# Cross attention with its scores two heads ahead of the transposes, and an output layer whose first block goes chunk by chunk

## The chip, the cores and the metric

One core of one Trainium2 chip runs the whole program in one launch. The metric is the device time of an execution in microseconds (us). The kernel before was timed three times; one more execution was recorded by the profiler.

## What is computed

The reference is a stack of two models over 512 tokens of width 1024. Each of the first model's two layers has a mixer, a cross attention over 256 memory rows, and a feed-forward part; the second model has two blocks of its own. The part that matters here is the cross attention, called once in each layer of the first model:

```python
def memory_cross_attention(h, mem_n, wq, wkv, wo):
    ...
    q = (h @ wq).reshape(B, S, XA_HEADS, XA_HEAD_DIM)
    k, v = jnp.split(mem_n @ wkv, 2, axis=-1)
    ...
    s = jnp.einsum('bshd,bmhd->bhsm', q, k).astype(jnp.float32) * (XA_HEAD_DIM ** -0.5)
    p = jax.nn.softmax(s, axis=-1).astype(v.dtype)
    return jnp.einsum('bhsm,bmhd->bshd', p, v).reshape(B, S, XA_WIDTH) @ wo

x = x + memory_cross_attention(rmsnorm(x, norm_xattn_g), mem_n, wq, wkv, wo)
```

## The kernel before

The program is a list of stages (`schedule`), and each engine runs its own function for each stage, in the order of the list. Engines meet only by semaphores. Around the change the list reads: the query layer (`xq`, two blocks), the attention (`xattn`, four heads), the output layer (`xo`, four blocks, which add to X), then the feed-forward part.

**Linear layers.** The activations lie with features on the partitions, in chunks of 128 features by 512 tokens. To keep float32 precision each operand is split into a hi and a lo part, and each product is three matmuls (`three`, L943 to L945): hi by hi, hi by lo, lo by hi. A block is 256 output features: two PSUM banks (m = 0, 1) of ACC, summed over the input chunks k. Blocks take turns on two pairs of banks, ACC[0:2] and ACC[2:4]. The weights arrive from memory in units of 1 MB over SP's queue (L841) into one of two RAW buffers; ACT makes the hi part (WH, L1620), VectorE (DVE) the lo part (WL, L2040). A unit of the output layer holds two of its blocks (`bpu` = 2), and its blocks are drained only when both are done (`unit_done`); DVE then adds them to X (L2119). The query layer's blocks are drained by DVE into XQ (L2097), 1024 values per partition at a time, which posts `block_done`.

A block normally runs over all k of bank 0 and then over all k of bank 1. The first block of a layer that opens behind a norm (`first_block`, L968 to L975) runs over k outside and the two banks inside, so that it can start on the first chunks. Either form waits for `h_ready` before it reads chunk k.

**Attention**, per head h, with the two buffers or bank pairs chosen by h % 2:

- scores (TensorE, L1075): four matmuls of 128x256 (the profile counts eight) into a pair of banks of ACC. For h = 0 it waits until both query blocks are drained; for h of 2 and 3 until the exponential has read the banks (`xs_exp`);
- maximum (DVE, L2291 and L2292), posts `xs_max`;
- exponential (ACT, L1738), four times 128x256 with a running sum, into XP, after the transposes of head h - 2 have read it (`xs_turned`);
- probabilities (DVE, L2297 and L2298): XP times the inverse of the sums, posts `xs_probs`;
- transposes (`turn`, TensorE, L1084): eight of 128x128 into the banks MIX[0:2], after the copy of head h - 1 has emptied them;
- copy (`copy_turned`, ACT, L1753) to XPT;
- output (TensorE, L1093): two matmuls (four in the profile) into MIX[2] or MIX[3];
- T (DVE, L2304), HH (`hi_chunks`, ACT, L1667) and HL (`lo`, DVE, L2308): the head's output as a chunk for the output layer, split in hi and lo; HL posts `h_ready`. T has two buffers, and the chunk after next waits until the lo part is made.

Each queue runs in the order written. Before, TensorE's is s0 s1 t0 s2 t1 o0 s3 t2 o1 t3 o2 o3 (s scores, t transposes, o output); ACT's is e0 e1 c0 e2 c1 hi0 e3 c2 hi1 c3 hi2 hi3 (e exponential, c copy); DVE's is m0 m1 p0 m2 p1 m3 p2 T0 lo0 p3 T1 lo1 T2 lo2 T3 lo3 (m maximum, p probabilities).

The MLA attention, elsewhere in the list, has eight heads in an order of the same kind: s0 s1 t0 s2 t1 o0 s3 t2 o1 and so on (L1492, L1506, L1515), with ten transposes a head.

Of the kernel before, what the change touches and what calls it, by code (L numbers as in the profile page):

```python
# [31 lines left out]
XH = 4  # L32
# [384 lines left out]
def build(nc, wall, xT, memT, params, consts, pos, poolw, params2, consts2, feats, decays, mats, filters, out):  # L417
# [7 lines left out]
    with ctx:  # L425
# [42 lines left out]
        T = place("T", [P, 2, S])  # L468
# [471 lines left out]
        def _(pe):  # L940
# [6 lines left out]
            def pe_linear(st):  # L947
# [4 lines left out]
                def period(i):  # L952
                    upp = 2 * st.upb
                    bpp = 2 * st.bpu
                    for j in in_period(st, i):
                        b = i * bpp + (st.b0 + j)
                        pair = (st.b0 + j) % 2
                        first_block = st.opens and isinstance(i, int) and i == j == 0
                        second_block = st.opens and isinstance(i, int) and i == 0 and j == 1
                        if not (isinstance(i, int) and b < 2):  # L960
                            pe.wait_ge(block_done, b - 1)
                        for q in range(st.upb):
                            ju = j * st.upb + q if st.bpu == 1 else j // st.bpu
                            n, add = unit_of(st, i, ju)
                            slot = n % 2
                            pe.wait_ge(w_lo, n + add + 1)
                            ks = range(8 * q, min(8 * q + 8, st.kc))
                            t0 = (j % st.bpu) * 2 * st.kc  # L968
                            if first_block and not tcs:
                                for k in ks:  # L970
                                    pe.wait_ge(h_ready, st.hin + k + 1)
                                    for m in range(2):
                                        c0 = (t0 + 2 * k + m) * P
                                        last = three(ACC[:, 2 * pair + m, :], WH[slot][:, c0:c0 + P], WL[slot][:, c0:c0 + P],
                                                     HH[:, k, :], HL[:, k, :], k == 0, k == st.kc - 1)  # L975
                            elif tcs:
                                for tc in range(tcs):
                                    if second_block and tc == 2:
                                        late_scale(st.norm)
                                    for k in ks:  # L980
                                        if tc == 0 and not st.whole:
                                            pe.wait_ge(h_ready, st.hin + k + 1)
                                        o = ACC[:, 2 * pair:2 * pair + 2, :].rearrange("p a (b n) -> p (a b) n", b=2)[:, tc]
                                        th, tl = HH[:, st.k0 + k, tc * P:tc * P + P], HL[:, st.k0 + k, tc * P:tc * P + P]
                                        c0 = (t0 + 2 * (k - 8 * q)) * P
                                        wh, wl = WH[slot][:, c0:c0 + 256], WL[slot][:, c0:c0 + 256]
                                        last = three(o, th, tl, wh, wl, k == 0, k == st.kc - 1)
                            else:
                                for m in range(1 if st.half and isinstance(i, int) and i * bpp + j == st.nb - 1 else 2):
                                    if second_block and m == 1:  # L990
                                        late_scale(st.norm)
                                    for k in ks:
                                        if m == 0 and src_h is HH and not st.whole:
                                            pe.wait_ge(h_ready, st.hin + k + 1)
                                        if m == 0 and src_h is HIDH:
                                            pe.wait_ge(hid_ready, st.hidin + k + 1)
                                        c0 = (t0 + 2 * (k - 8 * q) + m) * P
                                        last = three(ACC[:, 2 * pair + m, 0:width],
                                                     WH[slot][:, c0:c0 + P], WL[slot][:, c0:c0 + P],
                                                     src_h[:, st.k0 + k, 0:width], src_l[:, st.k0 + k, 0:width],  # L1000
                                                     k == 0, k == st.kc - 1)
                            if j % st.bpu == st.bpu - 1:
                                last.then_inc(unit_done, 1)
                        if first_block and st.norm.own == 2:
                            sum_paired(st.norm)
# [59 lines left out]
            def pe_xattn(st):  # L1065
                o = st.nth * XH

                def scores(h):
                    if h == 0:
                        pe.wait_ge(block_done, st.b0)  # L1070
                    if h >= 2:
                        pe.wait_ge(xs_exp, o + h - 1)
                    for tc in range(TC):
                        dst = ACC[:, 2 * (h % 2):2 * (h % 2) + 2, :].rearrange("p a (b n) -> p (a b) n", b=2)[:, tc]
                        mm = pe.matmul(dst, XQ[:, h, tc * P:tc * P + P], XK[:, h, :], start=True, stop=True)  # L1075
                    mm.then_inc(xs_scores, 1)

                def turn(h):
                    pe.wait_ge(xs_probs, o + h + 1)
                    if h >= 1:  # L1080
                        pe.wait_ge(xs_copied, o + h)
                    for mc in range(MC):
                        for tc in range(TC):
                            mm = pe.transpose(MIX[:, mc, tc * P:tc * P + P],  # L1084
                                              XP[:, h % 2, tc, mc * P:mc * P + P], ident)
                    mm.then_inc(xs_turned, 1)

                def output(h):
                    pe.wait_ge(xs_copied, o + h + 1)
                    if h >= 2:  # L1090
                        pe.wait_ge(t_ready, st.h0 + h - 1)
                    for mc in range(MC):
                        mm = pe.matmul(MIX[:, 2 + h % 2, :], XV[:, mc, h * P:h * P + P], XPT[:, h % 2, mc, :],  # L1093
                                       start=(mc == 0), stop=(mc == MC - 1))
                    mm.then_inc(xs_out, 1)

                scores(0)
                for h in range(XH):
                    if h + 1 < XH:
                        scores(h + 1)  # L1100
                    turn(h)
                    if h:
                        output(h - 1)
                output(XH - 1)

            def pe_prep(st):
                L = st.layer
# [502 lines left out]
        def _(act):  # L1610
# [118 lines left out]

            def act_xattn(st):  # L1730
                o = st.nth * XH
                for h in range(XH):
                    act.wait_ge(xs_max, o + h + 1)
                    if h >= 2:
                        act.wait_ge(xs_turned, o + h - 1)
# [2 lines left out]
                        a = act.activation(XP[:, h % 2, tc, :], src, ACT.Exp, bias=XS[:, h % 2, 0, tc:tc + 1],  # L1738
                                           scale=float(P) ** -0.5, accum_out=XS[:, h % 2, 1, tc:tc + 1])
                    a.then_inc(xs_exp, 1)  # L1740
                    if h:
                        copy_turned(st, h - 1)
                    if h >= 2:
                        hi_chunks(st.h0 + h - 2, [h - 2])
                copy_turned(st, XH - 1)
                hi_chunks(st.h0 + XH - 2, [XH - 2, XH - 1])

            def copy_turned(st, h):
                o = st.nth * XH
# [284 lines left out]
        def _(v):  # L2034
# [250 lines left out]
            def dve_xattn(st):  # L2285
                o = st.nth * XH

                def maximum(h):
                    v.wait_ge(xs_scores, o + h + 1)
                    src = ACC[:, 2 * (h % 2):2 * (h % 2) + 2, :].rearrange("p a (b n) -> p (a b) n", b=2)  # L2290
                    step(v.tensor_reduce(XS[:, h % 2, 2, :], src, AX.X, ALU.max))  # L2291
                    v.tensor_scalar(XS[:, h % 2, 0, :], XS[:, h % 2, 2, :], -float(P) ** -0.5, None, ALU.mult)\  # L2292
                        .then_inc(xs_max, 1)
# [12 lines left out]
                def lo(c):  # L2306
                    v.wait_ge(h_hi, st.h0 + c + 1)
                    v.tensor_tensor(HL[:, c, :], T[:, (st.h0 + c) % 2, :], HH[:, c, :], ALU.subtract).then_inc(h_ready, 1)  # L2308

                maximum(0)  # L2310
                for h in range(XH):
                    if h + 1 < XH:
                        maximum(h + 1)
                    probs(h)
                    if h >= 2:
                        produce(h - 2, T[:, (st.h0 + h - 2) % 2, :]).then_inc(t_ready, 1)
                        lo(h - 2)
                for c in (XH - 2, XH - 1):
                    produce(c, T[:, (st.h0 + c) % 2, :]).then_inc(t_ready, 1)
                    lo(c)  # L2320

            def dve_rope(st):
# [487 lines left out]
```

## Time and profile before

| | |
|---|---|
| median of three runs | 4165.9 us (4156.64 to 4167.36) |
| the profiled execution | 4161.2 us, its span 4159.4 us |
| mean granted TensorE clock | 0.952 |
| busy, share of the span | PE 92%, PE weight loads 74%, DVE 50%, ACT 26%, POOL 1% |
| first cross attention | about 265 to 299 us of the span |
| second cross attention | about 1156 to 1192 us of the span |

PE is TensorE, PEld its weight loads, DVE VectorE, ACT ScalarE, POOL GpSimd, SP the queue that loads the weights. L12 is line 12 of the kernel. A row of the chain is a piece of the work that ended last, followed back from the end; "issue" in it is time in which the engine waited for nothing that the profile shows. In a timeline, the bracket gives the engine's idle time before the instruction and what ended it. The granted clock is a share of 2.4 GHz; 0.50 is its lower level, 1.2 GHz.

### The profile page before, as it was taken

The page shows a single profiled execution, that of the slowest core. Times are in us where ns is not written, and L with a number is a line of the kernel's source. Part 1 is how long each engine was busy: PE and PEld are TensorE (multiplying, and loading weights), DVE is VectorE, ACT ScalarE, POOL GpSimd, SP SyncE. Part 2 cuts the span into 40 slices and gives each one's busy share as a digit, 9 for nine tenths or more (in the row PEclk, how much of TensorE's full clock was granted, in tenths as well). Part 3 has the DMA queues.
Part 4 walks back from the last instruction along what each step waited for, and adds up shares of the span by engine and source line. Part 5 has one row for each costly group of instructions (what it writes and reads, how often), then busy time and mean ns, then how long its engine had stood idle before and what let it go on. Part 6 is the DMA issues. An engine that isn't in the chain of part 4 may idle for free.

```text
span 4159.4 us, 42350 instructions
## 1 busy us (share of the span) xinstructions
PE 3829.6 (92%) x17182; PEld 3073.3 (74%) x17182; DVE 2068.1 (50%) x2589; ACT 1096.8 (26%) x1218; POOL 48.0 (1%) x65
## 2 busy tenths in 40 slices
PE   8889999978979998999998979999999998979998
PEld 6677888745758887888775757887888775857886
DVE  4555444363455434453656565444443656565433
ACT  2232222133332222222242312222222243312221
POOL 0000000000000000000000000000000000000000
PEclk9899999978999998999999989999999999989999
DMA  3122222210212221222312112222222312112221
GB/s 123 65 71 81 101 96 89 72 41 1 85 54 101 101 91 61 101 88 96 118 61 91 61 56 86 101 96 87 100 93 89 130 61 92 62 51 87 95 96 66
DMA packets 66781, 342.88 MB, mean 82 GB/s; under 512 B 23524, under 2 KB 23524, under 8 KB 30816
## 3 DMA queue, kind: packets, MB, share of 16 engines
q1 hardware_dynamic: 60864, 303.19, 20.9%
q0 software_dynamic: 5792, 37.92, 2.4%
q8 instruction: 91, 1.49, 0.2%
q14 instruction: 34, 0.28, 0.0%
HBM read 324.31 MB, written 16.78 MB: 82 GB/s over the span
## 4 chain that ended last, share of the span: by engine, by line
PE 83%; DVE 11%; ACT 2%; issue 2%; DMA 1%; SPq 0%; DVEq 0%; ACTq 0%
PE ACC L943 24%; PE ACC L945 24%; PE ACC L944 24%; PE MIX L1017 1%; PE ACC L1461 1%; PE ACC L1201 1%; DVE WL L2040 1%; PE MIX L1034 1%; DVE BX L2544 1%; DVE BT L2542 1%; PE ACC L1181 1%; PE MIX L1113 1%; DVE PT L2734 0%; DVE PT L2732 0%; DMA RAW<-wall 0%
## 5 line engine op out<-in xcount | busy, mean ns | idle before, releaser
L943 PE MATMUL ACC<-HH,WH 128*128 128x512 f32 (+1 forms) x3322 | 1317.9, 397 | 92.3 <-issue 27.8
L944 PE MATMUL ACC<-HL,WH 128*128 128x512 f32 (+1 forms) x3322 | 1302.5, 392 | 0.0
L945 PE MATMUL ACC<-HH,WL 128*128 128x512 f32 (+1 forms) x3322 | 1301.1, 392 | 0.0
L2040 DVE TENSOR_TENSOR WL<-RAW,WH 128x2048 fp32r<-128x2048 f32 x292 | 668.2, 2288 | 507.7 <-ACT WH L1620 506.8
L943 PEld LDWEIGHTS ACC<-HH,WH 128*128 128x128 f32 x3322 | 635.3, 191 | 254.0 <-issue 76.6
L944 PEld LDWEIGHTS ACC<-HL,WH 128*128 128x128 f32 x3322 | 636.1, 191 | 131.2 <-issue 3.1
L945 PEld LDWEIGHTS ACC<-HH,WL 128*128 128x128 f32 x3322 | 634.6, 191 | 132.0
L1620 ACT ACTIVATE WH<-RAW 128x2048 fp32r<-128x2048 f32 x292 | 556.2, 1906 | 596.6 <-PE ACC L945 592.2
L945 PE MATMUL ACC<-HIDH,WL 128*128 128x512 f32 x1056 | 421.3, 399 | 0.0
L944 PE MATMUL ACC<-HIDL,WH 128*128 128x512 f32 x1056 | 416.1, 394 | 0.0
L943 PE MATMUL ACC<-HIDH,WH 128*128 128x512 f32 x1056 | 414.0, 392 | 0.0
L2126 DVE TENSOR_TENSOR SG<-ACC,RS 128x512 f32<-128x512 f32 x132 | 91.3, 691 | 625.7 <-PE ACC L945 625.5
L1643 ACT ACTIVATE SG<-SG 128x512 f32<-128x512 f32 x132 | 83.5, 633 | 1078.1 <-DVE SG L2126 1078.1
L944 PEld LDWEIGHTS ACC<-HIDL,WH 128*128 128x128 f32 x1056 | 198.2, 188 | 51.7
L943 PEld LDWEIGHTS ACC<-HIDH,WH 128*128 128x128 f32 x1056 | 198.3, 188 | 47.0
L945 PEld LDWEIGHTS ACC<-HIDH,WL 128*128 128x128 f32 x1056 | 198.2, 188 | 45.8
L1667 ACT ACTIVATE HH<-T 128x512 fp32r<-128x512 f32 (+1 forms) x149 | 87.5, 605 | 299.6 <-DVE T L2211 181.2
L2119 DVE SCALAR_TENSOR_TENSOR X<-ACC,X 128x1024 f32<-128x1024 f32 x48 | 58.6, 1224 | 210.3 <-PE ACC L945 210.3
L1461 PE MATMUL ACC<-INV,ZS 128*128 128x256 f32 x256 | 69.8, 440 | 36.7 <-DVE ZS L2738 36.7
L2132 DVE TENSOR_TENSOR T<-T,SG 128x512 f32<-128x512 f32 x132 | 91.5, 693 | 16.8 <-ACT SG L1643 2.0
L2135 DVE TENSOR_TENSOR HIDL<-T,HIDH 128x512 f32 (+1 forms) x132 | 91.4, 693 | 15.2
L1461 PEld LDWEIGHTS ACC<-INV,ZS 128*128 128x128 f32 x256 | 56.8, 225 | 51.4 <-DVE ZS L2738 27.4
(474 smaller groups left out, 3011.7 us busy)
## 6 DMA issues: line engine op xcount, KB each, us to landing
RAW<-wall SPq DMA_DIRECT2D x261, 1024.0 KB, 4.8
RAW<-wall SPq DMA_DIRECT2D x24, 768.0 KB, 4.1
KR<-spectra POOLq DMA_DIRECT2D x4, 2048.0 KB, 9.4
x_kept<-X POOLq DMA_DIRECT2D x2, 2048.0 KB, 6.7
FWK<-mats POOLq DMA_DIRECT2D x4, 1024.0 KB, 5.3
spectra<-SQ POOLq DMA_DIRECT2D x8, 512.0 KB, 2.9
spectra<-T POOLq DMA_DIRECT2D x8, 512.0 KB, 3.5
X<-x_kept POOLq DMA_DIRECT2D x2, 2048.0 KB, 14.6
```

The costliest lines, as they stand in the source:

```text
L943: pe.matmul(out_ap, wh, hh, start=first, stop=False)
L944: pe.matmul(out_ap, wh, hl, start=False, stop=False)
L945: return pe.matmul(out_ap, wl, hh, start=False, stop=last)
L1461: mm = pe.matmul(ACC[:, m, 256 * p:256 * p + 256], ZS[:, fc, 2 * p + cs, m * P:m * P + P], INV[:, cs, p, fc, :], start=(fc == cs == p == 0 ...
L1620: act.activation(WH[n % 2][:], RAW[n % 2][:], ACT.Copy).then_inc(w_hi, 1)
L1643: act.activation(SG[:], SG[:], ACT.Silu).then_inc(silu_ready, 1)
L1667: act.activation(HH[:, d, 0:width], T[:, (h0 + c) % 2, 0:width], ACT.Copy).then_inc(h_hi, 1)
L2040: v.tensor_tensor(WL[n % 2][:], RAW[n % 2][:], WH[n % 2][:], ALU.subtract).then_inc(w_lo, 1)
L2119: v.scalar_tensor_tensor(x2, two, st.scale, x2, ALU.mult, ALU.add).then_inc(block_done, 1)
L2126: v.tensor_tensor(SG[:], two[:, 0, :], scale, ALU.mult).then_inc(gate_ready, 1)
L2132: step(v.tensor_tensor(T[:, j, :], T[:, j, :], SG[:], ALU.mult))
L2135: v.tensor_tensor(HIDL[:, bass.ds(off, 1), :], T[:, j:j + 1, :], HIDH[:, bass.ds(off, 1), :], ALU.subtract).then_inc(hid_ready, 1)
```

## The change

Three things change. In the attention, all three engines get an order written out by hand: TensorE's is s0 s1 s2 t0 s3 t1 o0 t2 o1 t3 o2 o3; ACT's is e0 e1 c0 e2 c1 e3 c2 hi0 c3 hi1 hi2 hi3; DVE's is m0 m1 p0 m2 p1 m3 p2 T0 p3 lo0 T1 lo1 T2 lo2 T3 lo3, with a wait for the probabilities of head h - 2 before the maximum of heads 2 and 3. Scores(0) waits for the first query block alone and scores(1) for the second. The first block of the output layer takes the chunk-by-chunk form.

```diff
--- before.py
+++ after.py
@@ -966,7 +966,7 @@
                             pe.wait_ge(w_lo, n + add + 1)
                             ks = range(8 * q, min(8 * q + 8, st.kc))
                             t0 = (j % st.bpu) * 2 * st.kc
-                            if first_block and not tcs:
+                            if (first_block or st.src == "h" and st.bpu == 2 and i == j == 0) and not tcs:
                                 for k in ks:
                                     pe.wait_ge(h_ready, st.hin + k + 1)
                                     for m in range(2):
@@ -1066,8 +1066,8 @@
                 o = st.nth * XH
 
                 def scores(h):
-                    if h == 0:
-                        pe.wait_ge(block_done, st.b0)
+                    if h < 2:
+                        pe.wait_ge(block_done, st.b0 - 1 + h)
                     if h >= 2:
                         pe.wait_ge(xs_exp, o + h - 1)
                     for tc in range(TC):
@@ -1095,13 +1095,17 @@
                     mm.then_inc(xs_out, 1)
 
                 scores(0)
-                for h in range(XH):
-                    if h + 1 < XH:
-                        scores(h + 1)
-                    turn(h)
-                    if h:
-                        output(h - 1)
-                output(XH - 1)
+                scores(1)
+                scores(2)
+                turn(0)
+                scores(3)
+                turn(1)
+                output(0)
+                turn(2)
+                output(1)
+                turn(3)
+                output(2)
+                output(3)
 
             def pe_prep(st):
                 L = st.layer
@@ -1729,7 +1733,8 @@
 
             def act_xattn(st):
                 o = st.nth * XH
-                for h in range(XH):
+
+                def exponents(h):
                     act.wait_ge(xs_max, o + h + 1)
                     if h >= 2:
                         act.wait_ge(xs_turned, o + h - 1)
@@ -1738,12 +1743,18 @@
                         a = act.activation(XP[:, h % 2, tc, :], src, ACT.Exp, bias=XS[:, h % 2, 0, tc:tc + 1],
                                            scale=float(P) ** -0.5, accum_out=XS[:, h % 2, 1, tc:tc + 1])
                     a.then_inc(xs_exp, 1)
-                    if h:
-                        copy_turned(st, h - 1)
-                    if h >= 2:
-                        hi_chunks(st.h0 + h - 2, [h - 2])
-                copy_turned(st, XH - 1)
-                hi_chunks(st.h0 + XH - 2, [XH - 2, XH - 1])
+
+                exponents(0)
+                exponents(1)
+                copy_turned(st, 0)
+                exponents(2)
+                copy_turned(st, 1)
+                exponents(3)
+                copy_turned(st, 2)
+                hi_chunks(st.h0, [0])
+                copy_turned(st, 3)
+                for c in range(1, XH):
+                    hi_chunks(st.h0 + c, [c])
 
             def copy_turned(st, h):
                 o = st.nth * XH
@@ -2287,6 +2298,8 @@
 
                 def maximum(h):
                     v.wait_ge(xs_scores, o + h + 1)
+                    if h >= 2:
+                        v.wait_ge(xs_probs, o + h - 1)
                     src = ACC[:, 2 * (h % 2):2 * (h % 2) + 2, :].rearrange("p a (b n) -> p (a b) n", b=2)
                     step(v.tensor_reduce(XS[:, h % 2, 2, :], src, AX.X, ALU.max))
                     v.tensor_scalar(XS[:, h % 2, 0, :], XS[:, h % 2, 2, :], -float(P) ** -0.5, None, ALU.mult)\
@@ -2307,16 +2320,21 @@
                     v.wait_ge(h_hi, st.h0 + c + 1)
                     v.tensor_tensor(HL[:, c, :], T[:, (st.h0 + c) % 2, :], HH[:, c, :], ALU.subtract).then_inc(h_ready, 1)
 
+                def chunk(c):
+                    produce(c, T[:, (st.h0 + c) % 2, :]).then_inc(t_ready, 1)
+
                 maximum(0)
-                for h in range(XH):
-                    if h + 1 < XH:
-                        maximum(h + 1)
-                    probs(h)
-                    if h >= 2:
-                        produce(h - 2, T[:, (st.h0 + h - 2) % 2, :]).then_inc(t_ready, 1)
-                        lo(h - 2)
-                for c in (XH - 2, XH - 1):
-                    produce(c, T[:, (st.h0 + c) % 2, :]).then_inc(t_ready, 1)
+                maximum(1)
+                probs(0)
+                maximum(2)
+                probs(1)
+                maximum(3)
+                probs(2)
+                chunk(0)
+                probs(3)
+                lo(0)
+                for c in range(1, XH):
+                    chunk(c)
                     lo(c)
 
             def dve_rope(st):
```

## Rows read from the trace of the kernel before

**Rows 1.** The page, part 4: shares of the chain that ended last, by engine.
```profile
PE 83%; DVE 11%; ACT 2%; issue 2%; DMA 1%; SPq 0%; DVEq 0%; ACTq 0%
```

**Rows 2.** Windows: busy us (x instructions), clock, DMA share and GB/s, both stages.
```profile
core 0: us, PE busy (x) PEld busy (x) DVE busy (x) ACT busy (x) POOL busy (x), PEclk, DMA share, GB/s
264.90:298.90 34.00, 23.68 (x91) 15.26 (x89) 17.11 (x25) 14.18 (x41) 0.00 (x0) 0.90 0.09 31
1155.80:1192.10 36.30, 23.90 (x92) 15.47 (x91) 17.48 (x25) 14.74 (x41) 0.00 (x0) 0.91 0.08 29
```

**Rows 3.** Chain in order of time (start us, us, what), first stage.
```profile
265.22 1.24 DVE XQ L2097
266.50 2.01 PE ACC L1075 x8
...
269.99 1.94 ACT XP L1738 x8
...
272.17 1.24 DVE XP L2298
...
274.54 1.74 PE ACC L1075 x8
276.31 1.24 DVE XS L2291
...
281.10 2.19 PE MIX L1093 x4
...
293.53 1.73 PE MIX L1093 x4
295.29 0.70 DVE T L2304
296.01 0.64 ACT HH L1667
...
298.67 0.70 DVE HL L2308
299.41 0.50 PE ACC L943
...
308.58 1.24 DVE X L2119
```

**Rows 4.** Chain in order of time, second stage.
```profile
1156.28 1.24 DVE XQ L2097
...
1170.19 1.97 PE MIX L1084 x8
1172.16 3.42 PE MIX L1093 x4
...
1201.25 1.24 DVE X L2119
```

**Rows 5.** Timeline (start, us, instruction, [idle before <-releaser]), first stage.
```profile
271.81 0.48 ACT L1738 ACTIVATE XP<-ACC,XS 128x256 f32<-128x256 f32 x1
...
273.45 1.09 PE L1084 MATMUL MIX<-CON,XP 128*128 128x128 f32 x8 [3.23 <-DVE XP L2298]
...
274.58 1.02 ACT L1753 ACTIVATE XPT<-MIX 128x1024 f32<-128x1024 f32 x1 [0.83 <-PE MIX L1084]
...
277.77 0.47 ACT L1738 ACTIVATE XP<-ACC,XS 128x256 f32<-128x256 f32 x1 [2.17 <-DVE XS L2292]
...
279.13 1.97 PE L1084 MATMUL MIX<-CON,XP 128*128 128x128 f32 x8 [2.86 <-DVE XP L2298]
```

**Rows 6.** Windows: query block, MLA attention, second stage, layer behind L1113.
```profile
245.00:253.00 8.00, 8.00 (x37) 6.60 (x36) 5.32 (x11) 2.59 (x3) 0.00 (x0) 1.00 0.24 67
935.00:940.00 5.00, 5.00 (x23) 3.00 (x22) 1.66 (x6) 2.40 (x9) 0.00 (x0) 1.00 0.00 0
1172.00:1176.00 4.00, 4.00 (x7) 1.84 (x7) 0.00 (x0) 1.02 (x1) 0.00 (x0) 0.50 0.00 0
2130.00:2140.00 10.00, 10.00 (x37) 7.95 (x38) 3.85 (x10) 1.64 (x1) 0.00 (x0) 0.50 0.01 2
```

## The prediction

> **What bounds the kernel.** The page's chain of waits is read first: TensorE is 83% of it and VectorE 11% [rows 1], so a stretch counts where TensorE waits or runs slowly. The change touches one kind of stretch, the four-head cross attention, run twice, so the windows over the two stages come next: from the end of the last query matmul to the last late chunk of the output layer they last 34.0 and 36.3 us with TensorE busy 23.7 and 23.9 [rows 2]. The rest, 10.3 and 12.4 us, is idle TensorE, and part of the busy time is at half clock. The chain in order of time says what TensorE waits for: per head a ladder of scores (PE L1075), maximum (DVE L2291), exponential (ACT L1738), probabilities (DVE L2298), transposes (PE L1084), copy (ACT L1753) and output (PE L1093), each beginning 0.02 to 0.04 us after the one before [rows 3]. Then the last two heads' results pass one by one over DVE, ACT and DVE, and the output layer's k=3 matmul waits for the last (298.67, then 299.41) [rows 3]. Nothing else has to give: all of it is on the chain.
>
> **Durations, full clock.** Scores 1.74 us, 2.01 after an idle stretch; transposes 1.09; one output 1.73 [rows 3]. Scores to exponential 1.46 (276.31 to 277.77, DVE); an exponential's start to the transposes 3.46 (269.99 to 273.45), of which 1.97 until DVE takes it over and 1.48 the probabilities; 1.82 until ACT starts the next exponential (269.99, 271.81); 2.82 from the start of the next head's maximum where DVE does that first (276.31 to 279.13); copy 1.02 [rows 3 to 5]. A chunk of output costs 0.70 (T), 0.66 (HH), 0.70 (HL) [rows 3]. An output-layer matmul is 0.228: 299.41 to 308.58 holds 39 of them, 0.50 for the first [rows 3].
>
> **The change, walked with these.** Time 0 is the end of the last query matmul; h are heads. Before, VectorE's drain of the second query block (1.24) came first and scores(0) began at 1.28 [rows 3]. Now scores(0) needs only the first block, drained long ago: PE 0 to 1.74. This order is not in the trace; 1.74 is from a run of scores behind other matmuls, 2.01 the other bound (+0.27). The drain ends at 1.27 beside it, so the wait of scores(1) costs nothing; were the drain first, it would cost 1.28. Scores(1) 1.74 to 3.48. Maximum(0) on DVE from 1.77, exp(0) 3.22 to 5.19, exp(1) 5.04 to 7.01. Scores(2) reuses the banks of head 0, so it waits for exp(0): 5.2 to 7.21. That wait, 1.7 us, is the only idle stretch of TensorE left. Probs(0) is ready at 6.67, so turn(0) is 0.54 later than it could be: 7.21 to 8.30; scores(3) 8.30 to 10.04. DVE does maximum(2) from 7.24 and probs(1) by 10.06: turn(1) 10.08 to 11.17, output(0) to 12.90. ACT: copy(0) 8.34 to 9.36, exp(2) from 9.30 (0.6 later than its maximum, behind the copy in ACT's queue) to 11.27, copy(1) to 12.23, exp(3) 12.2 to 14.15. DVE: maximum(3) from 10.07, probs(2) by 12.89. Turn(2) 12.90 to 13.99, output(1) to 15.72. Probs(3) by 15.63; turn(3) 15.72 to 16.81, output(2) to 18.54, output(3) to 20.27. From 5.2 on TensorE does not stop.
>
> The new xs_probs waits before maximum(2) and (3) sit behind those very operations in DVE's queue: probs(1) ends about 10.03, as scores(3) does (10.04), so they cost nothing. What waits behind them is probs(1) and (2), and any slip of DVE there reaches the transposes one to one.
>
> **The tail.** Hi and lo of chunk 0 move behind exp(3) and probs(3): T(0) is copied from 12.93 (output(2) needs it by 16.8), HH(0) from 15.05, and HL(0), done at 16.4, isn't needed before 20.3. Copy(3) 16.85 to 17.87, HL(1) done 19.2, HL(2) 21.3, HL(3) 23.4 (2.06 a chunk). The output layer starts at 20.3. In the old order k=3 comes after 9 matmuls, at 22.5, and would wait 0.9; chunk by chunk it comes after 18, at 24.6, 1.2 after HL(3). So this part is worth 0.9 us a stage beside the other (0.4 alone, the wait before 299.41), and nothing waits. That this form runs at full pace the trace shows: the query layer's first block has it, and 245 to 253 holds TensorE busy throughout at clock 1.00 [rows 6]. Both blocks' 48 matmuls end at 20.3 + 0.2 + 48 x 0.228 = 31.4, where DVE adds to X. The second weight unit's split follows HH(3) and HL(3) (1.9 and 2.3 us, with a wait of 1.1: about 27.5) and is needed at 32.7. SP's next load starts then, earlier by as much as all else; POOL has no part.
>
> **The sum.** Before, from 265.22 to the add at 308.58 is 43.4 us, and 1156.28 to 1201.25 is 45.0 [rows 3, 4]. Now 31.4 each: 12.0 + 13.5 = 25.5 us. About 1.3 and 2.6 us of it are half-clock losses before (1.97 for 1.09 of transposes; 2.19 and 3.42 for 1.73 of output [rows 3 to 5]). Behind the add everything runs as before. Bounds: TensorE's own work is 4 x (1.74 + 1.09 + 1.73) = 18.2, so with no idle at all 29.4: at most 29.5 us in all. Below: if those half-clock losses stay, 21.6.
>
> That upper bound can be checked against another reading. The windows' busy time counts matmuls that overlap or run at half clock, so idle time alone gives 10.3 + 12.4 = 22.7 of room, less than the 25.5. The Trainium skill (Trainium Kernel Development and Optimization, Performance Expectations) says that matmul busy time is a bad metric and that the busy share of the weight loads is a good one. Weight loads are busy 15.3 and 15.5 us there [rows 2], and 6.60 of 8.00 in a dense layer [rows 6]; by that estimate the work would fit into 18.5 and 18.8 us and leave 33.0 us to be had. The durations leave 29.5, as a score, output or transpose spends less of its time on its weights than the layer's matmuls do; I go by the durations.
>
> The clock: TensorE was idle 3.23 us and kept its clock (transposes in 1.09), and 2.86 us later on and lost it (1.97) [rows 5]; in the other stage outputs ran at 0.50, the 1.2 GHz level [rows 6]. Now the longest idle is 1.7 us. The MLA attention, whose heads are the same three kinds of TensorE instruction, but follow each other without long gaps, runs at 1.00 with TensorE busy 5.00 of 5 [rows 6]. So I take full clock.
>
> The profiled execution took 4161.2 us (span 4159.4); with 25.5 less 4135.7. It lies 4.7 below the median of the runs, 4165.9, and the four times have a mean of 4162.7. I take 4162.7 - 25 = 4138.
>
> **Rivals.** (A) DVE becomes the bound. From 7.2 to 15.6 it and TensorE meet within 0.1 us at turn(1), turn(2) and turn(3), so 0.25 us more at each of some eight hand-offs gives 2 us a stage: 21 us gained, 4142. For: no slack in the walk. Against: the hand-offs measure 0.02 to 0.04.
> (B) The clock still falls. At worst it did so here from 1170.19 to 1175.58 (transposes, then outputs: 5.4 us) [rows 4]. TensorE being the bound, one such stretch in each stage costs 2.7 us there: 20.1 gained, 4143; two in each 14.7, 4148. For: the 0.50 row [rows 6]. Against: the longest idle is 1.7 us instead of 2.86.
> (C) Most of the gain is given back: exp(h+2) still waits for turn(h), and if turn(0), pushed behind scores(2), slid the ladder, a pair of heads would go through exponential, probabilities, transposes and copy in series again (1.97 + 1.48 + 1.09 + 1.02 = 5.6). One pair a stage leaves 14 us (4148, still faster), both leave 3: 4160. Against: the slip in the walk is 0.54.
> (D) Slower, by the clock: half clock from scores(2) to the end of both output blocks. TensorE's work there is 14.8 + 11.1, so +25.9 a stage against 12.8 won: 26 us slower, 4189; it is a loss once half clock lasts over 12.8 us a stage. For: TensorE stood full of work at 0.50 for the whole 10 us from 2130, right behind the matmuls of PE L1113 [rows 6]. Against: in these stages it fell only behind idle stretches, and the MLA row, the same kinds of instruction, stays at 1.00.
> (E) The change doesn't do what it says: scores(2) can't start before exp(0), so it is "two ahead" only after 5.2. That is counted; if it sent scores behind the transposes again, only the head start (1.5 a stage) and 0.4 stay: 4159.
>
> **Chances.** The forecast 0.72, A 0.10, B 0.07, C 0.06, E 0.02, D 0.03. About 12.5 us (0.3%) is what a measurement of this kernel can tell from no change. The forecast, A and B are faster by more: 0.89. C and E 0.08, D 0.03. Range: the most the bounds allow, 29.5, with 6 us for where a median falls, gives 4127; B at its worst, or C in one pair of heads, with the 3 us by which the median shown lies above the mean, gives 4151.
>
> **What would show it.** Right: from the query drain's neighbour to the X add 31 to 32 us in both stages; one idle stretch of TensorE of about 1.7 before scores(2); transposes in 1.09 each; no wait before the k=3 matmul; PE L1084's wait for XP nearly gone. DVE and ACT busy times unchanged. Wrong: transposes at 1.97 or granted clock under 0.9 (B, D); idle before every turn (A, C); a new wait in the layers behind, which would give the gain back later.

## The result, and the profile after

The median fell from 4166.0 us (6 runs, 4156.64 to 4168.32) to 4139.2 (6 runs, 4134.78 to 4145.78): a ratio of 0.9944, 95% interval 0.9933 to 0.9955 (the two medians alone give 0.9936). A second comparison, against 11 runs of the kernel before, gave 0.9951 (0.9935 to 0.9967), with medians 19.9 us apart where they are 26.8 apart here. The forecast was 4138, with a gain of 25.5 us in the two stages.

The page of the profile after; its execution took 4140.6 us:

```profile
span 4138.8 us, 42354 instructions
...
PE 3829.5 (93%) x17182; PEld 3076.9 (74%) x17182; DVE 2067.0 (50%) x2589; ACT 1096.4 (26%) x1218; POOL 47.3 (1%) x65
...
PE 84%; DVE 11%; ACT 2%; issue 2%; DMA 1%; SPq 0%; DVEq 0%; ACTq 0%
```

The busy times are those of before (DVE 2068.1, ACT 1096.8): no work was added or taken away. Only the idle time went, and TensorE's share of the chain is a point higher [rows 1].

The first stage, in the chain in order of time (start us, us, what):

```profile
264.95 1.74 PE ACC L1075 x8
266.72 1.24 DVE XS L2304
268.18 1.94 ACT XP L1743 x8
270.17 2.01 PE ACC L1075 x8
272.20 1.24 DVE XS L2304
273.74 1.23 DVE XP L2311
275.07 1.24 DVE XS L2304
276.61 1.24 DVE XP L2311
277.89 1.09 PE MIX L1084 x8
...
280.70 0.91 PE MIX L1084 x8
281.61 3.43 PE MIX L1093 x8
285.05 0.23 PE ACC L943
...
296.01 1.24 DVE X L2130
297.29 0.50 PE ACC L943
...
308.53 1.24 DVE X L2130
```

The drain of the second query block, which the chain before began with (265.22), starts at 264.99 here and is off the chain: scores(0) and (1) follow the last query matmul at once. The ladder stands once, over scores(0), maximum(0), exp(0) and scores(2). From 272.20 to 277.89 the chain is VectorE's: maximum(2), probs(1), maximum(3) and probs(2) without a stop, with TensorE busy beside it. From 277.89 the chain is TensorE alone, through the outputs into the output layer (285.05), with no T, HH and HL in it [rows 3]. The X add comes 31.02 us after the drain's start, where it was 43.36.

The same for the second stage; its drain starts at 1151.94:

```profile
1151.90 1.74 PE ACC L1075 x8
...
1168.56 3.44 PE MIX L1093 x8
...
1182.97 1.24 DVE X L2130
```

It takes 31.03 us, against 44.97 [rows 4]. The two stages together won 12.34 + 13.94 = 26.3 us.

Windows (us, busy us of each engine, clock, DMA share, GB/s) over both attentions, from the last query matmul to the last output, and over all between the first X add and the second stage's drain:

```profile
264.95:285.04 20.09, 18.01 (x82) 12.10 (x81) 15.49 (x22) 13.03 (x39) 0.00 (x0) 1.00 0.12 51
1151.90:1171.99 20.09, 18.02 (x82) 12.09 (x81) 15.49 (x22) 13.03 (x39) 0.00 (x0) 1.00 0.12 47
296.01:1151.94 855.93, 781.93 (x3515) 621.58 (x3516) 389.16 (x498) 235.22 (x295) 0.74 (x1) 0.93 0.20 70
```

Both attentions are equal to 0.01 us and at full clock, where the stages of before had 0.90 and 0.91 [rows 2]. TensorE's timeline in the first (start, us, instruction, [idle before <-releaser]):

```profile
270.17 1.99 PE L1075 MATMUL ACC<-XK,XQ 128*128 128x256 f32 x8 [1.76 <-ACT XP L1743]
272.00 1.04 PE L1084 MATMUL MIX<-CON,XP 128*128 128x128 f32 x8
...
275.02 1.09 PE L1084 MATMUL MIX<-CON,XP 128*128 128x128 f32 x8 [0.26 <-DVE XP L2311]
```

There is one idle stretch, 1.76 us ahead of scores(2), and 0.26 at turn(1), which waits for probs(1) of the VectorE stretch above. All transposes take 1.09 or less; none is at the 1.97 of [rows 4].

**Where six microseconds went.** The spans of the two profiled executions differ by 20.6 us, not by 26.3. Outside of the two stages (each from drain to X add) the program took 4071.0 us before and 4076.7 after. Between the stages, in code that is the same, it rose by more than that: 847.7 us there before (308.58 to 1156.28), 855.9 after; the rest fell by 2.5. The experiments ask whether the change costs this or the granted clock does.

### The profile page after: what moved, and what is told of

It is laid out like the page before. It is cut to its first block, busy times and chain, and to the rows that moved or that the text cites. A ratio compares the mean times of both kernels' runs of the same rounds, so it can differ in the third digit from the quotient of the medians.

```text
span 4138.8 us, 42354 instructions
## 1 busy us (share of the span) xinstructions
PE 3829.5 (93%) x17182; PEld 3076.9 (74%) x17182; DVE 2067.0 (50%) x2589; ACT 1096.4 (26%) x1218; POOL 47.3 (1%) x65
## 4 chain that ended last, share of the span: by engine, by line
PE 84%; DVE 11%; ACT 2%; issue 2%; DMA 1%; SPq 0%; DVEq 0%; ACTq 0%
PE ACC L943 24%; PE ACC L945 24%; PE ACC L944 24%; PE MIX L1017 1%; PE ACC L1465 1%; PE ACC L1205 1%; DVE WL L2051 1%; PE MIX L1034 1%; DVE BX L2562 1%; DVE BT L2560 1%; PE ACC L1185 1%; PE MIX L1117 0%; DVE PT L2752 0%; DVE PT L2750 0%; DMA RAW<-wall 0%
```

## Experiments

Each edited kernel was profiled once; "the stretch" is the time from the start of the second query block's drain to the first X add of the output layer, in the first and the second stage. Line numbers differ a little between kernels.

**1. The attention's orders alone.** The output layer's first block has its old form:

```diff
-                            if (first_block or st.src == "h" and st.bpu == 2 and i == j == 0) and not tcs:
+                            if first_block and not tcs:
```

> The attention's new orders without the chunk-by-chunk block of the output layer. The stretch from the drain of the second query block to the first X add was 43.36 and 44.97 us before and 31.1 in both stages after. The theory of the walk: the k=3 matmul comes after 9 matmuls, 0.9 us before its chunk, so the stretch is 0.9 longer than after: 32.0 in both stages. Rival (the output layer's form brings the larger part): over 34.

32.13 and 32.16 us. The chain in order of time, first stage:

```profile
285.41 0.70 DVE HL L2321
...
286.16 0.50 PE ACC L943
...
295.33 1.23 DVE X L2130
```

TensorE waits for the last lo part (HL, from 285.41) and starts k=3 at 286.16; in the timeline it had idled for 0.8 us. In the chunk-by-chunk form that part is off the chain. So the form is worth 1.1 us a stage beside the new orders, a little more than the 0.9 of the walk.

**2. The chunk-by-chunk block alone**, the same line changed the other way in the kernel before.

> The chunk-by-chunk block alone, with the attention as before. The walk: only the 0.38 us wait before the k=3 matmul goes, with the 0.27 of a restart: the stretches are 42.7 to 43.0 and 44.3 to 44.6 us, against 43.36 and 44.97. Rival: the 9 matmuls now done ahead of the last chunk are won in full, 2.05 us: 41.3 and 42.9.

44.49 and 42.96 us: neither. The clock fell in both stages, but at other places than in the profile of before. The chain, first stage:

```profile
271.93 3.17 PE ACC L1075 x8
...
279.07 3.40 PE MIX L1093 x4
```

Scores(2) took 3.17 us instead of 1.74 and output(0) 3.40 instead of 2.19. The stretches themselves can't tell the two prices apart, as the form is worth less than such a shift. The rows of the chain can: take off what each row on it took beyond its time at full clock (here 1.43 and 1.68, with 1.72 for an output; in the second stage 0.88 for transposes at 1176.71 and 0.73 for output(0) at 1178.67), and 41.4 us are left in both stages. The same for the kernel before (0.88 and 0.47 in the first stage; 0.88, 1.70 and, for scores(3) at 1175.58, 0.38 in the second) leaves 42.0 in both, and run 7 measures 42.06. So by this estimate the form alone is worth 0.65 us a stage, the 0.38 of the wait and the 0.27 of the restart as the walk has it, and not 2.05.

**3. The early scores alone**, all orders as before:

```diff
-                    if h == 0:
-                        pe.wait_ge(block_done, st.b0)
+                    if h < 2:
+                        pe.wait_ge(block_done, st.b0 - 1 + h)
```

> Only the waits of scores(0) and scores(1) on the query blocks are changed; all orders as before. The walk: the whole ladder starts 1.5 us earlier (1.28 of the drain and 0.27 of a restart): 41.8 and 43.4 us if the clock falls where it did before; a fall at another place can move either by 1 to 3 us. Rival: the head start is lost at a later wait, 43.4 and 45.0 again.

44.82 and 43.58 us: a head start that didn't show in the time. The chain, first stage:

```profile
264.93 1.74 PE ACC L1075 x8
...
271.62 1.97 PE MIX L1084 x8
273.58 2.29 PE ACC L1075 x8
...
278.72 1.97 PE MIX L1084 x8
280.69 3.41 PE MIX L1093 x4
284.10 2.15 PE ACC L1075 x8
...
309.79 1.24 DVE X L2119
```

The ladder does start earlier (scores at once), but already turn(0) takes 1.97, and turn(1) and output(0) (3.41) are at half clock too: 10.2 us of half clock in each stage, where before had 6.8. Taking the excess of the chain's rows off as in run 2 (4.4 us here, 3.1 in the second stage) leaves 40.41 and 40.45, 1.6 less than the same reading of before. The start was won and the clock gave it back.

**4. The changed kernel without the early scores**, the same lines the other way.

> The changed kernel, but scores(0) waits for both query blocks again. The walk: everything up to the output layer is 1.5 us later: 32.6 in both stages. Rival (TensorE has slack, so the start is absorbed): 31.1 as after.

32.62 in both stages, as the walk has it:

```profile
262.81 1.24 DVE XQ L2108
264.09 2.01 PE ACC L1075 x8
...
295.43 1.24 DVE X L2130
```

Scores(0) waits for the drain (262.81, 1.24) and pays the restart (2.01 for 1.74): 1.6 us a stage.

**5. Hi and lo back in their old places**, with the rest as changed:

```diff
                 copy_turned(st, 1)
+                hi_chunks(st.h0, [0])
                 exponents(3)
                 copy_turned(st, 2)
-                hi_chunks(st.h0, [0])
+                hi_chunks(st.h0 + 1, [1])
                 copy_turned(st, 3)
...
                 chunk(0)
+                lo(0)
                 probs(3)
-                lo(0)
```

> The changed kernel with hi and lo of chunk 0 back ahead of exp(3) and probs(3), and hi of chunk 1 ahead of copy(3). The walk: hi(0) waits for T(0), done at 13.6 after the last query matmul, and exp(3) starts at 14.2 instead of 12.2, so probs(3) and turn(3) come 2 us later and TensorE is idle for it: 33.1 us from the drain to the X add in both stages, against 31.0. Rival (the place of hi and lo in the queues doesn't matter): 31.0.

33.08 in both stages. The chain, first stage:

```profile
263.54 1.74 PE ACC L1075 x8
...
276.46 0.70 DVE T L2318
...
277.72 1.93 ACT XP L1743 x8
...
296.66 1.24 DVE X L2131
```

T(0) is copied at 276.46, hi(0) follows on ACT (277.19), and exp(3) starts at 277.72, 14.18 us after the last query matmul, as worked out; turn(3) then waits for it. In the changed kernel exp(3) starts 12.12 us after that matmul, 2.06 earlier, so the place of hi(0) alone accounts for the 2.05 us; hi(1) and lo(0), moved with it, are not on the chain. A 0.63 us copy in the wrong place of ACT's queue costs 2.05 us a stage, as it makes exp(3) wait for another engine's output. This one execution took 4129.7 us, less than the changed kernel's 4140.6, although both its stages are 2 us longer: single times of this kernel can't size such an edit, the stretch can.

**6. Both kernels once more**, unchanged, to see what the rest of the program does.

> The kernel before, unchanged, once more. Between the first stage's X add and the second stage's query drain lie 847.7 us in the profile of before and 855.9 in the one after, in code that is the same. Theory: this is the granted clock (109 us at half clock there before, 126 after), and moves by some 10 us from execution to execution: here it is anything from 848 to 865 with the half clock to match, and the sum of the stretches outside of the two stages rises by 0.4 to 0.5 us for each us of half clock. Rival: the change costs the layers behind it 8 us: 848 again.

> The changed kernel, unchanged, once more. Theory: 31.0 us in both stages to 0.2, no half clock in them, and the stretch between them anywhere from 848 to 865 with its half clock. Rival: 856 again, as a cost of the change.

The kernel before: 43.37 and 44.96 us in the stages, 847.8 between them. The changed one: 31.03 and 31.03, 859.5 between. The stages repeat to 0.01 us. Between them the kernel before repeated too, and the changed one was 3.6 us longer than at first. Over the profiled executions of all kernels but that of run 8, whose stages are drained otherwise (the time outside of the two stages, and how much of it the granted clock was at its lower level, 1.2 GHz, by the trace's record of it):

```
execution                       us outside   of it at half clock
hi and lo in old places (5)       4061.8           362
before, once more (6)             4066.3           369
scores(2) in other banks (9)      4070.6           376
before                            4071.0           382
after, beside run 8               4074.9           389
after, once more (6)              4075.0           393
after                             4076.7           396
output layer alone (2)            4076.6           404
before, filled (7)                4083.2           407
no early scores (4)               4078.6           407
early scores alone (3)            4081.4           414
attention's orders alone (1)      4087.0           420
```

From the first row to the last, 58 us more at half clock go with 25.2 us more time, 0.43 for each, and the others lie within 3.4 us of that line, whether they have the change or not. Between the stages alone, kernels with the old attention order took 847.7 to 862.1 us (five executions) and those with the new one 848.1 to 864.7 (seven). Outside of both stages the means are 4075.7 and 4074.9 us. So the time there goes with TensorE's clock, and a cost of 8 us in the layers behind the stages is not seen over these kernels.

The rival doesn't fall altogether. Executions of one kernel lie closer together between the stages than those of different kernels: the kernel before gave 847.7 and 847.8, the rival's own figure, the changed one 855.9, 859.5 and 856.0. And over all times on record the mean is 4163.0 for the kernel before (21) and 4140.6 for the changed one (13): 22.4 us apart, 3.2 either way, where the stages won 26.3; on one chip alone, in the second comparison, the means are 20.7 apart. The granted clock of the whole execution has the same mean in both, 0.952, although the stages held 13.7 us of half clock before and none after. By that, some ten us more of half clock lie elsewhere in the changed kernel, at 0.43 about 4 us: an estimate from clocks given to three digits. Whether the change brings that about is not shown, nor why the clock falls more in one kernel's execution than in another's, in code that is the same.

**7. What the clock's part is.** The kernel before, with work in TensorE's idle stretches:

```diff
+                def filler():
+                    for tc in range(TC):
+                        pe.matmul(MIX[:, 3, 256 * (tc % 2):256 * (tc % 2) + 256], XQ[:, 0, 0:P], XK[:, 0, :], start=True, stop=True)
...
                     if h + 1 < XH:
                         scores(h + 1)
+                        filler()
                     turn(h)
```

> The kernel before, with four matmuls of 128x256 (as many as a head of scores, 1.74 us) into a free bank behind scores(1), (2) and (3), where TensorE waits for the probabilities for 2.9 to 3.2 us; their results aren't used. Theory: they end before the probabilities are there, so they cost nothing, and the clock stays at 1.00: the stretches are 43.4 and 45.0 less the half-clock losses of 1.3 and 3.0, so 42.0 in both. Then the order is worth 11 us a stage and the clock 1.3 and 3.0. Rival (the fall of the clock has another cause): 43 to 45 with half clock in it.

42.06 us in both stages. Windows over the first, and its chain:

```profile
262.73:280.00 17.27, 13.35 (x64) 10.59 (x65) 8.11 (x11) 7.73 (x26) 0.00 (x0) 1.00 0.14 57
280.00:304.79 24.79, 21.49 (x90) 14.93 (x88) 11.66 (x15) 8.00 (x15) 0.00 (x0) 1.00 0.12 43
```

```profile
262.73 1.24 DVE XQ L2102
...
270.96 1.09 PE MIX L1088 x8
...
276.64 1.09 PE MIX L1088 x8
...
304.79 1.24 DVE X L2124
```

The clock stays at 1.00, both transposes take 1.09, and the added matmuls cost nothing: TensorE is still idle for 1.50, 1.13 and 1.14 us behind them when the probabilities come. So the old order at full clock is 42.06 us, and the result splits: 42.06 - 31.03 = 11.0 us a stage for the order, 1.3 and 2.9 for the clock. What kept the clock up is shown too, in the two stages of this one execution: TensorE's idle stretches, filled. The whole run took 4169.2 us, since its 862.1 us between the stages hid the gain.

**8. A version that beats both.** The chain after still has TensorE waiting 1.3 us for the first X add (296.01, restart at 297.29), and later a second add waiting behind the first. Each block of the output layer is now drained by itself (the semaphore is one that the program no longer counts with at that point):

```diff
                             if j % st.bpu == st.bpu - 1:
                                 last.then_inc(unit_done, 1)
+                            else:
+                                last.then_inc(pool_ready, 1)
...
-                        v.wait_ge(unit_done, done_after(st, i, j))
+                        if st.bpu == 2 and j % 2 == 0:
+                            v.wait_ge(pool_ready, 4 + 2 * int(st.name[2]) + j // 2 + 1)
+                        else:
+                            v.wait_ge(unit_done, done_after(st, i, j))
```

> The changed kernel, and the output layer's blocks are added to X as each is done, instead of both of a weight unit together. Behind the second block TensorE waits 1.3 us for its banks (295.99 to 297.29 after), and the last add waits behind an add and the squares of the block before (308.53 to 312.02). Theory: both waits go, the first 1.3 and the second 3.5: from the query drain to the last X add 42.0 to 42.3 us against 47.0 after, so 9 to 10 us in both stages together, and the median near 4130. Rival (DVE is still busy with the second unit's lo part, to about 27.5, and the adds come late): only the 3.5, 43.5 us. The other rival: what follows the last add doesn't start earlier, 4139.

> The changed kernel, timed beside the one above. Theory: 31.0 us in both stages, the median 4139 within 5, the ratio to before 0.993 to 0.996.

The median is 4123.8 us (6 runs, 4120.06 to 4136.24), against 4141.0 (4134.98 to 4150.67) for the changed kernel and 4160.9 for the one before on the same chip; the ratio to before is 0.9906 (0.9892 to 0.9921), the changed kernel's 0.9951. The chain behind the second block:

```profile
305.35 1.23 DVE X L2135
...
308.68 0.76 PE ACC L943
```

The drain began at 263.34, so the last X add (305.35) comes after 42.0 us, where it was 47.0 (264.99 to 312.02). That is 5.0 a stage, 10 together, as expected; the median was expected near 4130, and of the 17 between the medians 7 are not the stages'. The mean clock of the six executions was 0.9535, where the changed kernel's 13 have 0.9522, which is some 12 us less at half clock. The two executions profiled side by side differ by 2.4 us only (4136.2 and 4138.7), and there the new one had 17.8 us more at half clock: 10.1 - 0.43 x 17.8 = 2.4. Whether the seven us are luck or the edit's was not tested.

**9. TensorE's last idle stretch.** Scores(2) goes to MIX[2:4], which nobody uses yet, and output(0) waits for exp(2) instead; maximum and exponential read scores(2) from there:

```diff
-                    if h >= 2:
+                    if h == 3:
                         pe.wait_ge(xs_exp, o + h - 1)
...
-                        dst = ACC[:, 2 * (h % 2):2 * (h % 2) + 2, :].rearrange(
+                        dst = (MIX[:, 2:4, :] if h == 2 else ACC[:, 2 * (h % 2):2 * (h % 2) + 2, :]).rearrange(
...
+                    if h == 0:
+                        pe.wait_ge(xs_exp, o + 3)
```

> The changed kernel, with scores(2) in the output's two banks instead of head 0's, so that it doesn't wait for exp(0) and TensorE's 1.7 us of idle ahead of it go. The walk with that: turn(0) 0.5 us earlier, then the probabilities set the pace, the last output ends at 19.85 instead of 20.27 and the X add comes at 30.6 against 31.0 in both stages. Rival (TensorE is the bound and its idle time is all to be had): 29.3.

30.60 and 30.58 us. The chain, first stage:

```profile
263.55 1.74 PE ACC L1075 x8
...
270.24 1.11 PE MIX L1084 x8
271.39 0.90 issue
272.29 1.94 ACT XP L1745 x8
...
294.18 1.24 DVE X L2132
```

Scores(2) no longer waits for exp(0), but turn(0) then waits for probs(0) (TensorE is idle for 1.51 us), and exp(2), at 272.29, stands in ACT's queue behind copy(0) (271.37), which waits for turn(0). Taking 1.76 us of idle time away ahead of scores(2) gave 0.4, as most of it came back one step later.

## Why the prediction was right

**The walk.** From time 0 (264.95) the trace has scores(2) at 5.22 (walk 5.2), maximum(2) at 7.25 (7.24), maximum(3) at 10.12 (10.07), turn(2) at 12.94 (12.90) and turn(3) at 15.75 (15.72). The last output ended at 20.10 instead of 20.27: turn(3) follows a matmul without a gap and added 0.91, not 1.09. What is off the chain came earlier than walked: exp(2) at 9.04 (9.30), HL(3) done at 22.9 (23.4). The X add was 0.4 us earlier than forecast, 31.0 for 31.4: those 0.17, and the 0.2 for a restart at the output layer, which wasn't paid, as TensorE came to it without a stop. This is why the stages gave 26.3 and not 25.5.

**Part by part.** Early scores: 1.5 a stage in the walk, 1.6 measured (run 4), and 1.6 in the old order by its rows (run 3). The chunk-by-chunk block: 0.9, measured 1.1 (run 1); alone 0.4 and the restart, 0.65 by its rows (run 2). Hi and lo behind exp(3) and probs(3): the prediction only placed them and put no price on it; they are worth 2.05 (run 5). The price of 1.74 for scores behind other matmuls was right, and 2.01 was the wrong bound. These single removals (1.6, 1.1 and 2.05) don't add up to the 11.0. The 6.2 left are TensorE's order and what the parts do together, by subtraction only: what TensorE's order alone is worth was not run.

**The clock.** Taken as 1.00 because the longest idle stretch would be 1.7 us; it was 1.76, and the traces show no half clock in any of 16 stages with the new order (eight executions), and some in each of eight stages with the old one, not filled (four executions). Run 7 shows that filling the idle time is enough, with the same kinds of instruction in the same order. The clock's 1.3 and 2.6 us before were sized from three rows; they are 1.3 and 2.9.

**The rivals.** A (DVE the bound): from 272.20 to 277.89 it is, maximum(3) waits for DVE to end probs(1) and not for scores(3); but it meets TensorE as closely as written, and costs it 0.26 us at turn(1), and no more. B and D (the clock): no stage shows it. C (the ladder slides): scores(2) ended and turn(0) followed 7.23 us after time 0 (walk 7.21), and nothing slid behind it. E: the change does what it says. The reading by the weight loads put 33.0 us of room in the stages, against 29.5 by durations. In the attention after, with TensorE idle for 2.1 of 20.09 us, weight loads are busy 12.10, 0.60, far from the 0.82 of a dense layer: here that measure shows room where there is little. And the 29.5 can't be had by taking away idle time at one place either (run 9).

**Where a step failed.** "Behind the add everything runs as before" holds for the order and not for the time: outside of the stages the program ran between 4061.8 and 4087.0 us in twelve executions of nine kernels, and over all times on record the gain is 22.4 us where the stages gave 26.3 (run 6). The prediction allowed 6 us for that and was made against the mean of four times, which was as well: against the profiled execution alone (4135.7) it would have been 3.5 off. Its last sum also takes 25 for the 25.5 that it had worked out; with 25.5 it gives 4137. The range held. That the median came within 1.2 us is in part luck: the stages won 0.8 more than forecast, the program as a whole less, and the second comparison's median was 4141.0.

## What to carry to other kernels

Where a chain of engines hands one head to the next, write down each step's duration and each queue's order, and walk them: here that placed the attention's steps on the chain within 0.2 us and the X add within 0.4, and showed that an operation that waits for another engine's result belongs behind whatever the critical engine needs next. Measure such an edit between two fixed instructions on the chain, and not by the whole program's time, of which the part outside of the stages moved by 25 us from kernel to kernel; but time the whole as well, since what is won in a stage can be lost in part elsewhere.

## What the runs showed of the hardware

TensorE's clock is a hidden term in both directions. Starting the scores 1.6 us earlier alone made the two stages no faster together (44.8 and 43.6 us against 43.4 and 45.0), as they held 10.2 us of half clock each instead of 6.8. Matmuls with an unused result, placed in idle stretches of 2.9 to 3.2 us, cost nothing and won 1.3 and 2.9 us.

At full clock the stages of the changed kernel repeat to 0.01 us over three executions (31.02 or 31.03 in all six), while six timings of that kernel spread over 15.7 us (4134.98 to 4150.67). Outside of the stages the program's time goes with its time at half clock, 0.43 us for each. Eight transposes behind an output cost 0.91 us where they follow without a gap (turn(3)), instead of the 1.09 they take from a standstill.
